# Four instead of two rounded weight buffers in a two-block transformer kernel, with a new order at its start

## The chip, the cores and the metric

The kernel runs on one core of one Trainium2 chip. Its time is the device time of one execution in microseconds. Before the change the median of three runs is 2723.0 us (2719.33 to 2724.44).

## The reference

Two transformer blocks are computed one after the other on one sequence of 256 tokens with a model width of 2048, all in float32. Each block has a modulation by a condition vector `c`, a mixer and a convolved feed-forward part of width 5632:

```python
mod = jax.nn.silu(c) @ w_ada[l] + b_ada[l]          # 2048 x 12288
shift_m, scale_m, gate_m, shift_f, scale_f, gate_f = jnp.split(mod[:, None, :], 6, axis=-1)
h = rms_norm(x, norm_mix_g[l]) * (1.0 + scale_m) + shift_m
proj = h @ w_in[l]
q, k, v, xs, z, bmat, cmat, dt_raw = jnp.split(proj, split_at, axis=-1)
...
mix = jnp.concatenate([attn, ssm], axis=-1) @ w_out[l]
x = x + gate_m * mix
h = rms_norm(x, norm_ffn_g[l]) * (1.0 + scale_f) + shift_f
x = x + gate_f * conv_ffn(h, w_up[l], conv_ffn_w[l], conv_ffn_b[l], w_down[l])
```

The first block's mixer has 8 attention heads with a relative bias and a state space part with 16 heads, whose time steps are `softplus(dt_raw + dt_bias)`. The second block's mixer has a recurrent part of 16 heads (8 pairs) with a state of 64 x 64 and a pooling part. A final norm ends each block.

## The kernel before, in words

**Weights.** All weights but the modulation's come as a stream of 376 units of 1 MB (128 partitions x 2048 values), numbered in the order of use. A unit goes through three steps. The SP queue loads it into `w_raw[:, u % 4]` (L362). ACT copies it, rounded, into `w_hi[:, u % 2]` (L1006 or L1011). DVE subtracts the copy and writes the rest into `w_lo[:, u % 4]`, which lies on the memory of `w_raw` (L1468 or L1472). The activations are split in the same way into `h_hi` and `h_lo`. PE then forms a product with three matmuls: high x high, high x low, low x high (L686 to L688), 48 for a unit. The counter `units_used` is u + 3 when unit u is done. The load of unit u waits for unit u - 4, and the rounded copy of unit u waits for unit u - 2, since there are two buffers.

**Modulation.** A row block of `w_ada` (1 MB) is multiplied by silu(c) and summed by one DVE instruction (L1484), which the text calls an `ada` sum; `ada_done` counts the sums. The first 32 sums, shift and scale of the first norm, come by the SP queue into the four slots of `first_raw` (L380), all later ones by the POOL queue into the two slots of `ada_raw` (L2012). The load of block q into `first_raw` waits for `ada_done >= q - 3`, that is until sum q - 4 is done; a load into `ada_raw` waits until the sum two before it is done. Each engine and each queue works in the order of its program, so whatever stands behind a waiting instruction waits too.

**Beginning.** The SP queue issues c, the parameters, two `ada` blocks, the constant `ones`, x, two `ada` blocks, units 0 and 1, the constants `ident` and `tri` and the bias table, and then for k = 2 to 15 the blocks 2k, 2k + 1 and unit k. ACT squares x, PE sums the squares (L683) once all three constants are there (`con_in >= 48`), and DVE and ACT make the norm's factor. Then a loop runs over k = 0 to 15, a turn for each tile of 128 channels. DVE's turn is:

```python
if k >= 2:
    first_ada(2 * k)
    first_ada(2 * k + 1)
...
# the channel's shift and gain, then tmp = x * gain * rstd
lo_unit(U_QK + k)
...
# h_lo[:, k] (L1597), once ACT has written h_hi[:, k]
```

ACT's turn is `h_hi[:, k]` and then `hi_unit(k + 1)`. PE multiplies unit k by tile k into all eight banks, which are q and k of the attention; ACT and DVE copy them to `qk` after unit 15.

**Input projection.** Eight chunks of four units follow (the first has one unit). In each, DVE writes the four `w_lo`, evacuates the chunk before (for chunks 1 to 3 with 12 convolution taps, L1616) and forms up to four `ada` sums, at places that the table `in1_ada` lists. After chunk 6's units it computes softplus by a series of 19 dependent instructions on 16 partitions (L1636 to L1648). State space part, attention and output projection follow. In attention, DVE forms four `ada` sums between the probabilities and the norm's variance (L1499).

**Second mixer.** `wkv_pe`, `wkv_act` and `wkv_dve` work on two head pairs at a time, i = 0 to 3. Five doubling steps (m, DVE L1386) invert a triangular matrix, a recurrence of four steps (q) carries the state, and the y phase normalizes the result. These steps are chains of small matmuls and DVE and ACT instructions, so PE has units of other projections between them (`pair(*units[n], ks=(a, b))` is the part a to b of unit n in eighths).

Of the kernel before, what the change touches and what calls it, by code (L numbers as in the profile page):

```python
# [20 lines left out]
P = 128  # L21
# [21 lines left out]
FFN_A, FFN_B = 12, 10  # L43
UNIT = 2048
# [122 lines left out]
def build_program(nc, a, out):  # L167
    with ExitStack() as ctx:
# [11 lines left out]
        w_hi = sb(ctx, "w_hi", [P, 2, UNIT], F32R)  # L180
# [8 lines left out]
        h_hi = sb(ctx, "h_hi", [P, KT, T], F32R)  # L189
        h_lo = sb(ctx, "h_lo", [P, KT, T], F32R)  # L190
# [9 lines left out]
        rstd = sb(ctx, "rstd", [P, 2, T])  # L200
        tmp = sb(ctx, "tmp", [P, 4, T])
# [5 lines left out]
        with ExitStack() as s:  # L207
            hid_hi = sb(s, "hid_hi", [P, 2 * FFN_A, T], F32R)
            hid_lo = sb(s, "hid_lo", [P, 2 * FFN_A, T], F32R)
            conv_y = sb(s, "conv_y", [P, 2, 4, T])  # L210
            silu_g = sb(s, "silu_g", [P, 2, T])
            prod = sb(s, "prod", [P, 2, T])
        with ExitStack() as s:
# [12 lines left out]
            with ExitStack() as t:  # L226
                bias = [sb(t, "bias", [P, 4, T]), bias_b]
                logit = [sb(t, "logit", [P, 4, 384]), logit_b]
                prob_t = [sb(t, "prob_t", [P, 4, 384]), prob_t_b]
# [3 lines left out]
            with ExitStack() as t:  # L233
# [4 lines left out]
                x_tok = sb(t, "x_tok", [P, 2, WIDTH])  # L238
                cb_t = sb(t, "cb_t", [P, 2, 384])
                lm = sb(t, "lm", [P, 4, 384])  # L240
        with ExitStack() as s:
# [15 lines left out]
            with ExitStack() as t:  # L257
# [9 lines left out]
                mv = [sb(t, f"mv{i}", [P, 2, 2, 64]) for i in range(2)]  # L267
# [3 lines left out]
        wtmp = [tmp, tmp_b]  # L271

# [84 lines left out]
        def _(sp):  # L357
# [150 lines left out]
        def wkv_pe(pe, mm, pair, i):  # L508
# [98 lines left out]
            for q in range(4):  # L607
# [15 lines left out]
                for s, g, b in both:  # L623
# [25 lines left out]
            if i != 2:  # L649
                pair(*units[5], ks=(0, 2))  # L650

# [3 lines left out]
            if i != 2:  # L655
                pair(*units[5], ks=(2, 4))
# [8 lines left out]
            if i != 2:  # L665
                pair(*units[5], ks=(4, 8))
# [5 lines left out]
        def _(pe):  # L672
# [17 lines left out]
            def chunk(u0, e0, n0, kind, n_all=UNITS, i0=0):  # L690
                def body(c, par_):
                    pe.wait_ge(act_evac, c + (e0 + 1))
                    pe.wait_ge(dve_evac, c + (e0 + 1))
                    for i in range(i0, 4):
                        pe.wait_ge(lo_ready, 4 * c + (u0 + i + 1))
                        pe.wait_ge(n_lo, min(n0 + (16 if kind == "tile" else 4 * i + 4), n_all))
                        w_h, w_l = w_hi[:, slot_of(i, u0) % 2], w_lo[:, slot_of(i, u0)]
# [24 lines left out]
            def down(u0, hc0, e_next, n):  # L722
# [4 lines left out]
                def body(b, first=False):  # L727
                    for i in range(4):
                        pe.wait_ge(hid_lo_s, 2 * b + (hc0 + i // 2 + 1))
                        pe.wait_ge(lo_ready, 4 * b + (u0 + i + 1))  # L730
                        w_h, w_l = w_hi[:, slot_of(i, u0) % 2], w_lo[:, slot_of(i, u0)]
# [17 lines left out]
            def pair(u, n, k0, first, n0=None, ks=(0, 8)):  # L749
# [4 lines left out]
                w_h, w_l = w_hi[:, u % 2], w_lo[:, u % 4]  # L754
# [10 lines left out]
            def lora_tile(i):  # L765
                u = U_LORA + i
                pe.wait_ge(lo_ready, u + 1)
                w_h, w_l = w_hi[:, u % 2], w_lo[:, u % 4]
# [8 lines left out]
            pe.wait_ge(con_in, 48)  # L777
            stat(0)
            for k in range(KT):
                pe.wait_ge(n_lo, N_H1 + k + 1)  # L780
                pe.wait_ge(lo_ready, U_QK + k + 1)
                w_h, w_l = w_hi[:, k % 2], w_lo[:, k % 4]
# [13 lines left out]
            pe.wait_ge(S("decays"), 1)  # L796
            for j in range(4):
# [108 lines left out]
        def wkv_act(act, A, hi_unit, evac, i):  # L906
# [42 lines left out]
            for m in range(5):  # L949
# [10 lines left out]
                if m == 2:  # L960
                    for s, g, b in both:
                        act.wait_ge(S("mv_mm"), g + 1)
                        nc.scalar.copy(mv[s][:].rearrange("p a b v -> p (a b v)"), ps[:, b, 0:T]).then_inc(S("mv"), 1)
# [32 lines left out]
        def _(act):  # L996
# [3 lines left out]
            def hi(c, i, u0):  # L1000
# [4 lines left out]
                act.wait_ge(units_used, 4 * c + (u0 + i + 1))  # L1005
                nc.scalar.copy(w_hi[:, slot % 2], w_raw[:, slot]).then_inc(hi_ready, 1)  # L1006
# [58 lines left out]
            stat(0, xs, 0)  # L1065
            hi_unit(U_QK)
            hi_unit(U_QK + 1)
            root(0)
# [388 lines left out]
        def _(dve):  # L1457
# [5 lines left out]
            def lo(c, i, u0):  # L1463
# [113 lines left out]
            for q in range(4):  # L1577
# [3 lines left out]
            for k in range(KT):  # L1581
                if k >= 2:
# [48 lines left out]
            def softplus():  # L1631
# [3 lines left out]
                dve.wait_ge(S("dt_exp"), 2)  # L1635
                steps.link(ts(SV, EV, 2.0, None, ALU.add))  # L1636
                steps.link(V.reciprocal(SV, SV))
                steps.link(tt(SV, SV, EV, ALU.mult))
                steps.link(tt(S2, SV, SV, ALU.mult))
                steps.link(ts(EV, S2, 1.0 / 19.0, None, ALU.mult))  # L1640
                for k in range(8, 0, -1):
                    steps.link(stt(out=EV, in0=EV, scalar=1.0 / (2 * k + 1), in1=S2, op0=ALU.add, op1=ALU.mult))
                steps.link(stt(out=EV, in0=EV, scalar=1.0, in1=SV, op0=ALU.add, op1=ALU.mult))
                steps.link(ts(XV, XV, 0.0, None, ALU.max))
                steps.link(stt(out=dtcs[:, 0], in0=EV, scalar=2.0, in1=XV, op0=ALU.mult, op1=ALU.add))
                steps.link(ts(SV, dtcs[:, 0], NA, -1.0, ALU.mult, ALU.mult))
                steps.link(V.memset(S2, 1.0))
                V.tensor_tensor_scan(dtcs[:, 1], S2, SV, 0.0, ALU.mult, ALU.add).then_inc(S("decays"), 1)  # L1648
# [9 lines left out]
            in1_ada = ((0, 0, 0, 1), (1, 1, 1, 1), (0, 1, 1, 1), (0, 1, 1, 1), (0, 1, 1, 1), (1, 1, 1, 1), (0, 1, 0, 1),  # L1658
                       (1, 1, 1, 1))
            for c in range(8):  # L1660
# [9 lines left out]
                if c == 6:  # L1670
                    softplus()
# [462 lines left out]
```

## Time and profile before

| | |
|---|---|
| median of 3 runs | 2723.0 us |
| runs | 2719.33, 2723.0, 2724.44 us |
| profiled execution | 2718.6 us |
| its span, first to last instruction | 2716.7 us |
| mean granted TensorE clock | 0.951 |

The profile is that of one execution, and its times count from the first instruction. PE is TensorE, DVE is VectorE, ACT is ScalarE, POOL is GpSimd; SPq is the queue in which SyncE issues transfers. A clock of 1.00 is 2.4 GHz and one of 0.50 is 1.2 GHz. A releaser, shown as `<-`, is what ended an engine's wait.

### The profile page before, as it was taken

How to read it: one execution, taken by the hardware profiler on the slowest of the kernel's cores; microseconds unless marked ns; L12 is line 12 of the kernel's file. 1: busy time of each engine (PE TensorE's matmuls, PEld its weight loads, DVE VectorE, ACT ScalarE, POOL GpSimd, SP SyncE). 2: the span in 40 equal slices, each digit the busy share in tenths (PEclk: the TensorE clock that was granted, in tenths of full speed). 3: DMA queues.
4: the chain of work that ended last, by engine and by line, in shares of the span. 5: the costliest groups of instructions: out<-in, count | busy, mean ns of one | idle time of the engine just before them, and what ended most of it. 6: DMA issues, size and time to landing. Idle time of an engine off the chain costs nothing.

```text
span 2716.7 us, 51420 instructions
## 1 busy us (share of the span) xinstructions
PE 2491.7 (92%) x21636; PEld 2411.4 (89%) x21636; DVE 1883.8 (69%) x2215; ACT 1114.1 (41%) x1179; POOL 87.8 (3%) x184
## 2 busy tenths in 40 slices
PE   4889885989999999999979999899899999999997
PEld 4888854989999999999969888789899999999997
DVE  5988768877777677776769766667777654555544
ACT  3234323345554334443343445333555433344433
POOL 0000000000000000000000000000000000000000
PEclk9999966999999999999989999899899999999999
DMA  7987723957776887777938422216576545455442
GB/s 318 392 337 278 283 115 134 367 219 278 278 287 242 332 287 275 277 278 282 329 138 325 159 85 85 99 64 235 213 270 243 184 171 185 170 186 178 177 171 108
DMA packets 87914, 613.56 MB, mean 226 GB/s; under 512 B 9576, under 2 KB 13168, under 8 KB 14320
## 3 DMA queue, kind: packets, MB, share of 16 engines
q1 hardware_dynamic: 64608, 442.95, 44.6%
q0 software_dynamic: 23184, 168.83, 16.1%
q8 instruction: 95, 1.56, 0.2%
q14 instruction: 27, 0.22, 0.0%
HBM read 607.54 MB, written 4.21 MB: 225 GB/s over the span
## 4 chain that ended last, share of the span: by engine, by line
PE 81%; DVE 12%; ACT 3%; issue 2%; DMA 1%; SPq 0%; DVEq 0%; ACTq 0%
PE ps L686 24%; PE ps L688 24%; PE ps L687 24%; DVE first_raw L1484 2%; PE ps L683 2%; DVE w_lo L1472 2%; ACT w_hi L1011 1%; DMA tri<-in_consts 1%; PE ps L573 1%; DVE w_lo L1468 1%; PE ps L818 1%; DVE rstd L1503 1%; PE ps L467 1%; DVE tmp L1511 1%; DVE xbc L1616 1%
## 5 line engine op out<-in xcount | busy, mean ns | idle before, releaser
L686 PE MATMUL ps<-h_hi,w_hi 128*128 128x256 f32 x4480 | 1288.3, 288 | 78.9 <-DVE h_lo L1597 28.3
L688 PE MATMUL ps<-h_hi,w_lo 128*128 128x256 f32 x4480 | 1278.6, 285 | 0.0
L687 PE MATMUL ps<-h_lo,w_hi 128*128 128x256 f32 x4480 | 1278.5, 285 | 0.0
L1468 DVE TENSOR_TENSOR w_lo<-w_raw,w_hi 128x2048 fp32r<-128x2048 f32 x307 | 703.7, 2292 | 534.8 <-ACT w_hi L1006 531.0
L1006 ACT CAST w_hi<-w_raw 128x2048 fp32r<-128x2048 f32 x306 | 583.5, 1907 | 1005.2 <-PE ps L688 972.2
L686 PEld LDWEIGHTS ps<-h_hi,w_hi 128*128 128x128 f32 x4480 | 871.2, 194 | 90.2 <-issue 33.6
L687 PEld LDWEIGHTS ps<-h_lo,w_hi 128*128 128x128 f32 x4480 | 871.6, 195 | 0.4
L688 PEld LDWEIGHTS ps<-h_hi,w_lo 128*128 128x128 f32 x4480 | 870.4, 194 | 0.0
L686 PE MATMUL ps<-hid_hi,w_hi 128*128 (+1 forms) x1408 | 397.3, 282 | 21.8 <-issue 21.8
L687 PE MATMUL ps<-hid_lo,w_hi 128*128 (+1 forms) x1408 | 396.6, 282 | 0.0
L688 PE MATMUL ps<-hid_hi,w_lo 128*128 (+1 forms) x1408 | 396.4, 282 | 0.0
L1484 DVE SCALAR_TENSOR_TENSOR ada_raw<-ada_raw,ada_c 128x2048 f32<-128x2048 f32 x160 | 365.3, 2285 | 9.1 <-DMA ada_raw<-in_ada_stream 9.1
L686 PEld LDWEIGHTS ps<-hid_hi,w_hi 128*128 128x128 f32 x1408 | 268.5, 191 | 22.5 <-issue 22.5
L687 PEld LDWEIGHTS ps<-hid_lo,w_hi 128*128 128x128 f32 x1408 | 268.5, 191 | 0.0
L688 PEld LDWEIGHTS ps<-hid_hi,w_lo 128*128 128x128 f32 x1408 | 268.3, 191 | 0.0
L1472 DVE TENSOR_TENSOR w_lo<-w_raw,w_hi 128x2048 fp32r<-128x2048 f32 x69 | 157.9, 2290 | 56.7 <-ACT w_hi L1011 56.2
L1011 ACT CAST w_hi<-w_raw 128x2048 fp32r<-128x2048 f32 x70 | 133.3, 1905 | 119.5 <-PE ps L688 114.8
L1784 DVE SCALAR_TENSOR_TENSOR conv_y<-ps,par,conv_y 128x254 f32<-128x254 f32 (+1 forms) x352 | 145.2, 475 | 18.8 <-ACT conv_y L1156 13.8
L2012 POOL DMA_DIRECT2D ada_raw<-in_ada_stream x160 | 84.6, 529 | 1940.0 <-DVE ada_raw L1484 1792.2
L683 PE MATMUL ps<-tmp,ones 128*128 128x256 f32 x224 | 65.9, 458 | 53.2 <-DMA tri<-in_consts 27.8
L683 PEld LDWEIGHTS ps<-tmp,ones 128*128 128x128 f32 x224 | 50.9, 233 | 64.6 <-DMA tri<-in_consts 27.8
L1156 ACT ACTIVATE conv_y<-ps,par 128x256 f32<-128x256 f32 x176 | 84.9, 563 | 15.2 <-PE ps L688 15.2
(331 smaller groups left out, 1531.8 us busy)
## 6 DMA issues: line engine op xcount, KB each, us to landing
w_raw<-in_w_stream SPq DMA_DIRECT2D x376, 1024.0 KB, 4.8
ada_raw<-in_ada_stream POOLq DMA_DIRECT2D x160, 1024.0 KB, 6.8
first_raw<-in_ada_stream SPq DMA_DIRECT2D x32, 1024.0 KB, 7.4
x<-in_x_t SPq DMA_DIRECT2D x1, 2048.0 KB, 13.8
x_kept<-x SPq DMA_DIRECT2D x1, 2048.0 KB, 7.3
out_t<-x SPq DMA_DIRECT2D x4, 512.0 KB, 2.7
ada_c<-in_c SPq DMA_DIRECT2D x1, 1024.0 KB, 4.4
ada_c<-in_c POOLq DMA_DIRECT2D x1, 1024.0 KB, 6.1
```

The source lines that it names most:

```text
L683: mm(bank(b), ones[:], tmp[:, q % 4], start=k == 0, stop=k == STATS[s] - 1).then_inc(sq_used, 1)
L686: mm(o, hi, r_hi, start=first, stop=False, **kw)
L687: mm(o, hi, r_lo, start=False, stop=False, **kw)
L688: return mm(o, lo, r_hi, start=False, stop=last, **kw)
L1006: nc.scalar.copy(w_hi[:, slot % 2], w_raw[:, slot]).then_inc(hi_ready, 1)
L1011: nc.scalar.copy(w_hi[:, u % 2], w_raw[:, u % 4]).then_inc(hi_ready, 1)
L1156: last = A(conv_y[:, par_, i], bank(4 * par_ + i), ACT.Identity, bias=pc(par_name, o + 3), scale=pc(par_name, o + 2))
L1468: tt(w_lo[:, slot], w_raw[:, slot], w_hi[:, slot % 2].bitcast(F32), ALU.subtract).then_inc(lo_ready, 1)
L1472: tt(w_lo[:, u % 4], w_raw[:, u % 4], w_hi[:, u % 2].bitcast(F32), ALU.subtract).then_inc(lo_ready, 1)
L1484: stt(out=rows, in0=rows, scalar=1.0, in1=ada_c[:], op0=ALU.mult, op1=ALU.mult, accum_out=col(mod, pair)).then_inc(ada_done, 1)
L1784: last = stt(out=conv_y[:, par_, i, d:T], in0=ps[:, 4 * par_ + i, 0:T - d], scalar=pc(par_name, o + 2 - d), in1=conv_y[:, par_, i, d:T], o ...
L2012: G.dma_start(ada_raw[:, slot], src).then_inc(ada_loaded[slot], 16)
```

## The change

`w_hi` gets four slots, so unit u has slot u % 4 in all three tiles, and a rounded copy waits for unit u - 4. For the memory, `prod` moves under `tmp`, `x_tok` and one `prob_t` under `h_lo`, and `mv` becomes a part of `wtmp`.

At the beginning the order of loads is new, PE's statistics wait for `ones` alone, DVE forms eight instead of four `ada` sums ahead of the loop and none in turns 0 to 3, and ACT takes the root ahead of the first two rounded copies. `first_raw` keeps its four slots and `load_first_ada` its wait.

Softplus is cut into three parts, put behind units (5, 3), (6, 0) and (6, 3). One `ada` sum leaves chunk 5, one moves within chunk 6, and attention gets a fifth. In the second mixer the sixth unit moves from the y phase into the four steps of the recurrence (for i = 0, 1 and 3).

```diff
-        w_hi = sb(ctx, "w_hi", [P, 2, UNIT], F32R)
+        w_hi = sb(ctx, "w_hi", [P, 4, UNIT], F32R)
...
+        with ExitStack() as under:
+            x_tok = sb(under, "x_tok", [P, 2, WIDTH])
+        with ExitStack() as under:
+            prob_t_a = sb(under, "prob_t", [P, 4, 384])
         h_lo = sb(ctx, "h_lo", [P, KT, T], F32R)
...
+        mv = [t[:, 1].rearrange("p (a b v) -> p a b v", a=2, b=2) for t in wtmp]
...
             sp.dma_start(ada_c[:], a["c"].partition_broadcast(P)).then_inc(c_in, 16)
-            sp.dma_start(par[:], a["params"]).then_inc(par_in, 16)
-            load_first_ada(0)
-            load_first_ada(1)
             sp.dma_start(ones[:], a["consts"][:, CCOL["ones"]:CCOL["ones"] + P]).then_inc(con_in, 16)
             sp.dma_start(x[:], a["x_t"]).then_inc(x_in, 16)
-            load_first_ada(2)
-            load_first_ada(3)
+            sp.dma_start(par[:], a["params"]).then_inc(par_in, 16)
+            for q in range(4):
+                load_first_ada(q)
             load_w(U_QK, 0, True)
-            load_w(U_QK + 1, 1, True)
+            for q in range(4, 2 * AHEAD):
+                load_first_ada(q)
+            for k in range(1, KT):
+                load_w(U_QK + k, k % 4, k < 4)
+                if k + AHEAD - 1 < KT:
+                    load_first_ada(2 * (k + AHEAD - 1))
+                    load_first_ada(2 * (k + AHEAD - 1) + 1)
             sp.dma_start(ident[:], a["consts"][:, CCOL["ident"]:CCOL["ident"] + P]).then_inc(con_in, 16)
             sp.dma_start(tri[:], a["consts"][:, CCOL["tri"]:CCOL["tri"] + T]).then_inc(con_in, 16)
             sp.dma_start(relb[:], a["rel_bias"]).then_inc(relb_in, 16)
-            for k in range(2, KT):
-                load_first_ada(2 * k)
-                load_first_ada(2 * k + 1)
-                load_w(U_QK + k, k % 4, k < 4)
...
+                if i != 2:
+                    pair(*units[5], ks=(2 * q, 2 * q + 2))
                 if q == 3:
                     break
...
-            if i != 2:
-                pair(*units[5], ks=(0, 2))
...
-            if i != 2:
-                pair(*units[5], ks=(2, 4))
...
-            if i != 2:
-                pair(*units[5], ks=(4, 8))
...
-            pe.wait_ge(con_in, 48)
+            pe.wait_ge(con_in, 16)
             stat(0)
...
             def hi_unit(u):
                 act.wait_ge(w_loaded[u % 4], 16 * (u // 4 + 1))
-                act.wait_ge(units_used, u + 1)
-                nc.scalar.copy(w_hi[:, u % 2], w_raw[:, u % 4]).then_inc(hi_ready, 1)
+                if u >= 4:
+                    act.wait_ge(units_used, u - 1)
+                nc.scalar.copy(w_hi[:, u % 4], w_raw[:, u % 4]).then_inc(hi_ready, 1)
...
             stat(0, xs, 0)
+            root(0)
             hi_unit(U_QK)
             hi_unit(U_QK + 1)
-            root(0)
...
-            for q in range(4):
+            for q in range(2 * AHEAD):
                 first_ada(q)
             var(0, D)
             inverse(0)
             for k in range(KT):
-                if k >= 2:
+                if k >= AHEAD:
                     first_ada(2 * k)
                     first_ada(2 * k + 1)
...
+            SOFTPLUS = {(5, 3): 0, (6, 0): 1, (6, 3): 2}
-            in1_ada = ((0, 0, 0, 1), (1, 1, 1, 1), (0, 1, 1, 1), (0, 1, 1, 1), (0, 1, 1, 1), (1, 1, 1, 1), (0, 1, 0, 1),
+            in1_ada = ((0, 0, 0, 1), (1, 1, 1, 1), (0, 1, 1, 1), (0, 1, 1, 1), (0, 1, 1, 1), (1, 1, 1, 0), (0, 1, 1, 0),
                        (1, 1, 1, 1))
...
-                if c == 6:
-                    softplus()
+                    if (c, i) in SOFTPLUS:
+                        softplus(SOFTPLUS[c, i])
...
-            next_ada(4)
+            next_ada(5)
```

`AHEAD` is 4. The same change of `hi_unit` is made in `hi`, and all readers of `w_hi` take slot u % 4.

## Rows read from the trace of the kernel before

**Rows 1.** Page, parts 1 and 2: span, and each engine's busy time (share) xinstructions.

```profile
span 2716.7 us, 51420 instructions
...
PE 2491.7 (92%) x21636; PEld 2411.4 (89%) x21636; DVE 1883.8 (69%) x2215; ACT 1114.1 (41%) x1179; POOL 87.8 (3%) x184
```

**Rows 2.** Waits of PE, whole span: engine line <- releaser: us in total, times, longest.

```profile
PE ps L686 <- DVE h_lo L1597: 28.3, 14, 9.3
PE ps L683 <- DMA tri<-in_consts: 27.8, 1, 27.8
...
PE ps L716 <- DVE w_lo L1468: 7.5, 1, 7.5
...
PE ps L686 <- DVE w_lo L1468: 6.6, 3, 2.2
```

**Rows 3.** Windows: width, busy us of PE, PEld, DVE, ACT, POOL, PEclk, DMA share, GB/s.

```profile
20.00:40.00 20.00, 10.22 (x32) 8.15 (x32) 4.77 (x5) 8.24 (x14) 2.49 (x19) 1.00 1.01 418
68.00:148.00 80.00, 65.88 (x494) 63.85 (x493) 79.31 (x91) 24.68 (x21) 0.00 (x0) 0.94 1.00 396
330.00:337.00 7.00, 6.77 (x21) 5.52 (x22) 7.00 (x5) 0.00 (x0) 0.53 (x1) 0.69 0.41 136
```

**Rows 4.** Timeline of DVE, one turn of the first loop: start, us, engine line op.

```profile
59.64 2.29 DVE L1484 SCALAR_TENSOR_TENSOR first_raw<-first_raw,ada_c 128x2048 f32<-128x2048 f32 x1
...
64.91 2.28 DVE L1472 TENSOR_TENSOR w_lo<-w_raw,w_hi 128x2048 fp32r<-128x2048 f32 x1
67.11 0.48 DVE L1597 SCALAR_TENSOR_TENSOR h_lo<-tmp,mod,h_hi 128x256 fp32r<-128x256 f32 x1
67.50 2.28 DVE L1484 SCALAR_TENSOR_TENSOR first_raw<-first_raw,ada_c 128x2048 f32<-128x2048 f32 x1
```

**Rows 5.** Timeline of the SP queue, first loop, turn k = 4's issues.

```profile
52.87 2.54 SPq L380 DMA_DIRECT2D first_raw<-in_ada_stream  x2
55.45 0.43 SPq L362 DMA_DIRECT2D w_raw<-in_w_stream  x1
```

**Rows 6.** Tile w_raw, 50 to 58 us: landing of the weight issued at 55.45.

```profile
DMA to landing us min/median/max: 8.7/8.7/8.7
```

**Rows 7.** DMA issues, first 1.3 us: KB each, us to landing.

```profile
ada_c<-in_c SPq DMA_DIRECT2D x1, 1024.0 KB, 4.4
```

**Rows 8.** Timeline of ACT: x has landed; third rounded copy; end of unit 15.

```profile
17.26 1.33 ACT L1024 ACTIVATE tmp<-x 128x256 f32<-128x256 f32 x4 [10.08 <-DMA x<-in_x_t]
...
55.10 1.90 ACT L1011 CAST w_hi<-w_raw 128x2048 fp32r<-128x2048 f32 x1 [6.52 <-PE ps L688]
...
168.08 1.93 ACT L1076 COPY qk<-ps 128x1024 f32<-128x1024 f32 x2 [5.91 <-PE ps L688]
```

**Rows 9.** Timeline of PE: start of unit 0.

```profile
47.36 0.58 PE L686 MATMUL ps<-h_hi,w_hi 128*128 128x256 f32 x1 [9.32 <-DVE h_lo L1597]
```

**Rows 10.** Timeline of DVE, chunk 2 of the input projection.

```profile
200.46 2.29 DVE L1468 TENSOR_TENSOR w_lo<-w_raw,w_hi 128x2048 fp32r<-128x2048 f32 x1 [3.45 <-ACT w_hi L1006]
202.67 5.02 DVE L1616 SCALAR_TENSOR_TENSOR xbc<-ps,par,xbc 128x255 f32<-128x255 f32 x12
```

**Rows 11.** Timeline of DVE, chunk 6: softplus, its longest step and the w_lo behind it.

```profile
318.60 1.74 DVE L1637 RECIPROCAL sp_w<-sp_w 16x256 f32<-16x256 f32 x1
...
327.72 2.25 DVE L1468 TENSOR_TENSOR w_lo<-w_raw,w_hi 128x2048 fp32r<-128x2048 f32 x1
```

**Rows 12.** Timeline of DVE, end of attention: last two sums, then variance.

```profile
454.68 2.29 DVE L1484 SCALAR_TENSOR_TENSOR ada_raw<-ada_raw,ada_c 128x2048 f32<-128x2048 f32 x1 [3.53 <-DMA ada_raw<-in_ada_stream]
...
457.67 2.29 DVE L1484 SCALAR_TENSOR_TENSOR ada_raw<-ada_raw,ada_c 128x2048 f32<-128x2048 f32 x1 [0.69 <-DMA ada_raw<-in_ada_stream]
...
460.68 0.42 DVE L1499 TENSOR_SCALAR rstd<-ps 128x256 f32<-128x256 f32 x1 [0.71 <-PE ps L683]
```

**Rows 13.** Timeline of DVE, fourth doubling step, i=1 and i=2.

```profile
1640.88 0.42 DVE L1386 TENSOR_TENSOR inv_t<-inv_t,ps 128x256 f32<-128x256 f32 x1 [1.39 <-PE ps L603]
...
1724.83 0.42 DVE L1386 TENSOR_TENSOR inv_t<-inv_t,ps 128x256 f32<-128x256 f32 x1 [3.94 <-PE ps L603]
```

More of the change, by code:

```diff
@@ L200, in build_program @@
         rstd = sb(ctx, "rstd", [P, 2, T])
+        with ExitStack() as under:
+            prod = sb(under, "prod", [P, 2, T])
         tmp = sb(ctx, "tmp", [P, 4, T])
@@ L228, in build_program @@
                 logit = [sb(t, "logit", [P, 4, 384]), logit_b]
-                prob_t = [sb(t, "prob_t", [P, 4, 384]), prob_t_b]
+                prob_t = [prob_t_a, prob_t_b]
                 att_m = [sb(t, f"att_m{b}", [P, 8]) for b in range(2)]
@@ L696, in body @@
                         pe.wait_ge(n_lo, min(n0 + (16 if kind == "tile" else 4 * i + 4), n_all))
-                        w_h, w_l = w_hi[:, slot_of(i, u0) % 2], w_lo[:, slot_of(i, u0)]
+                        w_h, w_l = w_hi[:, slot_of(i, u0)], w_lo[:, slot_of(i, u0)]
                         if kind == "tile":
@@ L730, in body @@
                         pe.wait_ge(lo_ready, 4 * b + (u0 + i + 1))
-                        w_h, w_l = w_hi[:, slot_of(i, u0) % 2], w_lo[:, slot_of(i, u0)]
+                        w_h, w_l = w_hi[:, slot_of(i, u0)], w_lo[:, slot_of(i, u0)]
                         for j in range(16):
@@ L753, in pair @@
                 pe.wait_ge(lo_ready, u + 1)
-                w_h, w_l = w_hi[:, u % 2], w_lo[:, u % 4]
+                w_h, w_l = w_hi[:, u % 4], w_lo[:, u % 4]
                 for k in range(*ks):
@@ L767, in lora_tile @@
                 pe.wait_ge(lo_ready, u + 1)
-                w_h, w_l = w_hi[:, u % 2], w_lo[:, u % 4]
+                w_h, w_l = w_hi[:, u % 4], w_lo[:, u % 4]
                 o = ps[:, (C_LORA + i // 2) % 2, (i % 2) * T:(i % 2) * T + T]
@@ L781, in _ @@
                 pe.wait_ge(lo_ready, U_QK + k + 1)
-                w_h, w_l = w_hi[:, k % 2], w_lo[:, k % 4]
+                w_h, w_l = w_hi[:, k % 4], w_lo[:, k % 4]
                 for j in range(16):
@@ L962, in wkv_act @@
                         act.wait_ge(S("mv_mm"), g + 1)
-                        nc.scalar.copy(mv[s][:].rearrange("p a b v -> p (a b v)"), ps[:, b, 0:T]).then_inc(S("mv"), 1)
+                        nc.scalar.copy(wtmp[s][:, 1], ps[:, b, 0:T]).then_inc(S("mv"), 1)
             for q in range(4):
@@ L1629, in in1_evac, with softplus @@
                     V.tensor_copy(v_tok[:, 1, o:o + 512], ps[:, 4 * par_ + 1, :]).then_inc(dve_evac, 1)
-            def softplus():
+            def softplus(part):
                 XV, EV, SV, S2 = (sp_w[:, i] for i in range(4))
                 NA = sp_w[:, 4, 0:1]
[L1635 to L1648, printed above, removed]
@@ new lines, in softplus @@
+                if part == 0:
+                    dve.wait_ge(S("dt_exp"), 2)
+                    steps.link(ts(SV, EV, 2.0, None, ALU.add))
+                    steps.link(V.reciprocal(SV, SV))
+                    steps.link(tt(SV, SV, EV, ALU.mult))
+                    steps.link(tt(S2, SV, SV, ALU.mult))
+                    steps.link(ts(EV, S2, 1.0 / 19.0, None, ALU.mult))
+                elif part == 1:
+                    for k in range(8, 0, -1):
+                        steps.link(stt(out=EV, in0=EV, scalar=1.0 / (2 * k + 1), in1=S2, op0=ALU.add, op1=ALU.mult))
+                else:
+                    steps.link(stt(out=EV, in0=EV, scalar=1.0, in1=SV, op0=ALU.add, op1=ALU.mult))
+                    steps.link(ts(XV, XV, 0.0, None, ALU.max))
+                    steps.link(stt(out=dtcs[:, 0], in0=EV, scalar=2.0, in1=XV, op0=ALU.mult, op1=ALU.add))
+                    steps.link(ts(SV, dtcs[:, 0], NA, -1.0, ALU.mult, ALU.mult))
+                    steps.link(V.memset(S2, 1.0))
+                    V.tensor_tensor_scan(dtcs[:, 1], S2, SV, 0.0, ALU.mult, ALU.add).then_inc(S("decays"), 1)
```

13 lines of the change are left out of this document (6 added, 7 removed).

## The prediction

> **What bounds the kernel now.** I read the page's busy shares first: PE works 92% of a span of 2716.7 us [rows 1]. So the change can save only where PE stands idle, and can lose wherever something else comes to set PE's pace. The list of PE's waits says where it stands idle. It names the constant `tri` (27.8 us in one piece, at the very start), `h_lo` of line 1597 (28.3 us over 14 waits, the first loop over `w_in`'s q and k columns), softplus in front of a `w_lo` (7.5 us) and three stalls of 2.2 us, 6.6 together, in the input projection [rows 2]. In the long streams of the feed-forward parts PE waits for no rounded weight at all. There a rounded copy that is ready earlier is worth nothing.
>
> The windows and timelines of the first 170 us then show what the new order acts on. From 68 to 148 us DVE is busy 79.31 of 80 us, while PE has 65.88 and the DMA engines are full [rows 3]. A turn of that loop takes 7.86 us (59.64 to 67.50). DVE forms two `ada` sums, then the small gain operations, starts `lo_unit` 5.27 us into the turn and `h_lo` 7.47 us into it [rows 4]. PE needs less per unit and waits.
>
> **The change, part by part.**
>
> *The start.* In the trace, `x` lands at 17.26 us behind 5780 KB (c, parameters, ones, two `ada` blocks and itself) [rows 8]. At the 418 GB/s of a full stretch [rows 3] these are 14.2 us, so 3.1 us lie around them. In the new order the eighth `ada` block is behind 12948 KB and lands at 31.7 + 3.1 = 34.8 us. DVE has summed it at 37.1, and statistics, root and reciprocal follow. Statistics no longer wait for `tri`, but the eighth sum comes later than they end, so only part of the 27.8 us comes back. `w3` is behind another 7168 KB and lands at 52.4. Its rounded copy (1.90 [rows 8]), `w_lo` (2.20, 64.91 to 67.11 [rows 4]) and `h_lo` (0.4) bring DVE to turn k = 4 at 56.9 us. Before it is 67.50 [rows 4]. Gain: 10.6 us. Four sums have moved out of the loop into time in which DVE waited, and turns 0 to 3 carry none.
>
> *The steady turns.* Here I expect the loss. The SP queue is in order, and I followed it against DVE's order. SP issues for k = 1, 2, ...: `load_w(k)`, then `ada` 2k+6 and 2k+7. But `first_raw` still has four slots, so `load_first_ada(q)` waits until sum q-4 is done. `ada` 2k+7 waits for sum 2k+3, which is the second sum of turn k+1. `load_w(k+1)` stands behind it in the queue. So from k = 4 on, `w_k` is issued only after both sums of turn k, and DVE's next large instruction in that same turn is `lo_unit(k)`, which needs `w_k` landed and rounded. In the kernel before, `w_k` stands behind `ada` 2k+1 instead, which waits for a sum of turn k-2, two turns of slack.
>
> The price of one such turn comes from a burst that the trace already has. At 52.87 and at about 55.1 us two `ada` blocks are issued into empty queues as sums finish, and the weight at 55.45, 2.58 us after the first [rows 5]. It lands 8.7 us after its issue, behind those two blocks [rows 6]. The first issue follows the first sum's start by 2.33 us (a sum is 2.29 [rows 4]). So in a new turn the weight is issued at 2.33 + 2.58 = 4.91 and lands at 13.6. The rounded copy adds 1.9 (15.5), `w_lo` 2.2 (17.7), `h_lo` 0.4 and two hand-overs make it 18.2 us against 7.86. This holds for k = 4 to 13, ten turns. After k = 12 no `ada` loads are left, so `w14` and `w15` are issued right behind `w13`, and turns 14 and 15 are of the old kind. Loss: 10 x (18.2 - 7.86) = 103.4 us. Nothing covers it: PE has each unit done within the turn, and four rounded buffers don't help, since no raw weight is there to be rounded.
>
> The bounds: if the two blocks ahead cost the weight nothing, it lands as the lone 1024 KB transfer of the start does, in 4.4 us [rows 7]. The turn is then 13.9 and the loss 60 us. From above, SP may issue or the blocks may land a little later: 1 us a turn more, 113 us. I take the burst, since it is the same sequence of three issues into idle queues.
>
> The Trainium skill (DMA: Bandwidth & Descriptors, Anatomy of one DMA) says that DMA engines don't wait on semaphores and that any wait is held on the issuing sequencer before dispatch, which is why a waiting `ada` load holds the weight behind it; it gives about 2.0 us fixed plus bytes at 436 GB/s. By that estimate three blocks from 2.33 us on would land at 2.33 + 2.0 + 7.2 = 11.5 us, a turn of 16.1 and a loss of 82 us. The row's 13.6 stands against it, and the sum goes by the row.
>
> *The last unit.* Unit 0 starts at 47.36 [rows 9] and is over when ACT is released at 55.10 [rows 8]: 7.7 us, from an idle PE. Unit 15 now takes 6.0 (`h_lo` of turn 15 starts at 67.50 + 11 x 7.86 + 7.47 = 161.4, PE 0.6 later, ACT is released at 168.08 [rows 8]). PE will idle some 10 us in every new turn, so I give the last unit 7.7: +1.7 us. The stage ends at 56.9 + 182 + 15.7 + 7.8 = 262.4 instead of 168.1. So +94.5 us in all, which is also -10.6 + 103.4 + 1.7.
>
> *Four rounded buffers in the input projection.* In a chunk with convolution DVE's `w_lo` at 200.46 waited 3.45 us for ACT's rounded copy, which waited for PE; then come 5.02 us of taps, and the `w_lo` behind them is late [rows 10]. With two more buffers that copy and its `w_lo` (1.9 + 2.2) are done before the chunk ends, so the taps start 2.2 us earlier (ACT's own part of the evacuation, 1.9, is then ahead of them). That removes 2.1 of each 2.2 us stall: -6.3.
>
> *Softplus in three parts.* Today it is a block on DVE, from before 318.60 to the next `w_lo` at 327.72 [rows 11], about 9.4 us, and PE waits 7.5 [rows 2]. Split over two chunks of some 22 us, in which DVE has 4 x 2.2 for weights and 2 or 3 sums, it fits: -7.5. The clock granted in 330 to 337 us is 0.69 [rows 3], behind that idle stretch; 0.31 / 0.5 x 7 = 4.3 us at 1.2 GHz cost 2.2 us, which come back: -2.2.
>
> *The fifth sum in attention.* The sums of `ada` there are paced by the POOL queue: the third starts at 454.68 after waiting 3.53 us for its block, the fourth at 457.67, and the variance follows at 460.68 [rows 12]. There are two slots, so a block is loaded only when the sum two before it is done. The second sum ended at 454.68 - 3.53 = 451.15 and the first 2.2 earlier, so these two blocks took 5.7 and 6.5 us. A fifth is issued at 454.68 + 2.3 = 457.0 and takes 6.2; its sum ends at 465.5. The variance sits behind it in DVE's order, and PE behind the norm: 465.5 - 460.7 = +4.8 us. The sum that was taken out of chunk 5 gives nothing, since DVE has slack there.
>
> *The sixth unit.* Its 48 matmuls move from the y phase into the four steps of the state recurrence, for i = 0, 1, 3. What such filler costs in a chain is shown by one doubling step: with 24 matmuls in it (i = 2) DVE waits 3.94 us, without (i = 1) 1.39 [rows 13]; so 24 cost 2.55 us, 48 about 5.1. What leaves the y phase is 5.8 us of PE time, of which its own waits hid some 2 to 3; a clock that stays up in the recurrence gives about 2 back. Net between -2 and +2 per i; I take +1 for all.
>
> *Memory and the rest.* `x_tok`, `prob_t` and `prod` lie on memory whose users have finished by the orders already there, and `mv` becomes a part of `wtmp`, dead at that step: 0. `ident`, `tri` and the bias table load after turn 15, some 90 us ahead of use: 0.
>
> **Sum.** +94.5 - 6.3 - 7.5 - 2.2 + 4.8 + 1 = +84.3 us. The profiled execution took 2718.6 us, of which 1.9 lie around the span; the median of the runs is 2723.0. The first gives 2803, the second 2807; I say 2805 us, +3.0%.
>
> **Rivals.** *A, faster: the order doesn't bind.* If `w_k` were issued in time (a sum of turn k did not stand ahead of it), the loop would keep 7.86 us per turn, and the rest would be -10.6 - 6.3 - 7.5 - 2.2 + 4.8 + 1 = -20.8: 2702 us. It decides when the weight is issued before about -1 us in its turn (4.4 + 1.9 before 5.27). For it speaks only that two loads of slack are there for k = 1 to 3; against it speaks the count of sums above. Chance 0.05. *B: the turn is short.* The weight lands in 4.4 us, the turn is 13.9, the loss 60 instead of 103: 2762 us. For it, the DMA queues are empty when the turn begins; against it, the 8.7 us of the burst [rows 6]. Values between come with it. Chance 0.14. *C: lost and won in balance.* Only a few turns wait, DVE catches up, and the time stays within 0.2%: it would take a stall of 2 us a turn where 10 are worked out. Chance 0.01. The forecast, 2785 to 2825 us, has 0.80.
>
> **The numbers.** The range of 8 in 10 takes the forecast and most of B: 2763 to 2825 us. The upper end has 1 us a turn more and half of the input projection's gains missing. Within 0.2%, about 5 us, is what measurement can't tell from no change. Faster 0.05, same 0.01, slower 0.94.
>
> **What would show it.** In the timeline of SP, ten weight issues 18 us apart, each right behind an `ada` issue. In DVE's idle time, about ten waits of 10 us for `w_hi`, and for `w_hi` a wait for the DMA of `w_raw`. The first copy of `qk` by ACT near 262 us, turn 4 near 57. No 2.2 us stalls and no 7.5 us stall behind it, and some 5 us more of idle PE ahead of the output projection. I am wrong if SP's weight issues come 8 us apart, or if the traffic lands much faster than the burst did.

## The result, and the profile after

The changed kernel takes 2783.55 us (median of 4 runs, 2780.39 to 2785.31), the kernel before 2721.16 us beside it: a ratio of 1.0227, with a 95% interval of 1.0209 to 1.0245. It is 62 us slower. The forecast was 2805 us, with a range of 2763 to 2825.

The page of the profiled execution (2780.39 us), which answers to [rows 1], with its chain that ended last:

```profile
span 2778.4 us, 51419 instructions
...
PE 2493.7 (90%) x21636; PEld 2415.7 (87%) x21636; DVE 1873.8 (67%) x2215; ACT 1112.0 (40%) x1179; POOL 99.2 (4%) x184
...
PE 78%; DVE 11%; DMA 5%; ACT 4%; issue 2%; SPq 0%; DVEq 0%; POOLq 0%; ACTq 0%
PE ps L686 23%; PE ps L687 23%; PE ps L688 23%; DMA w_raw<-in_w_stream 4%; DVE first_raw L1486 2%; PE ps L683 2%; ACT w_hi L1013 1%; DVE w_lo L1474 1%; DMA first_raw<-in_ada_stream 1%; PE ps L578 1%; PE ps L819 1%; PE ps L472 1%; DVE tmp L1513 1%; DVE xbc L1618 1%; PE ps L718 1%
```

The work is the same: no engine's busy time moved by more than 12 us, and the span grew by 61.7. So the loss is waiting. The chain says what for: the load of a weight, `w_raw`, is 4% of the span, and it isn't in this list of the kernel before. PE's waits, the answer to [rows 2]:

```profile
PE ps L686 <- DVE h_lo L1599: 111.6, 12, 21.9
...
PE ps L686 <- DVE w_lo L1470: 0.5, 1, 0.5
```

The wait for `tri`, the 7.5 us and the three of 2.2 us are gone. `h_lo` of the first loop has grown from 28.3 to 111.6 us. One of these waits, 21.9 us, is for the first tile, where PE waited for `tri` before; the others are those of the slow turns. The window over that loop's slow part, in the columns of [rows 3]:

```profile
57.00:230.00 173.00, 85.42 (x532) 83.39 (x530) 78.60 (x91) 24.74 (x21) 0.00 (x0) 0.72 0.50 194
```

DVE does in 173 us what it did in 80: the same 91 instructions, 78.60 us of work against 79.31 [rows 3]. The DMA engines work half of the time, and PE's clock is down to 0.72. Why no engine is busy is seen in one turn, followed over three timelines. First the SP queue, the answer to [rows 5]:

```profile
59.46 2.54 SPq L385 DMA_DIRECT2D first_raw<-in_ada_stream  x2
62.05 0.43 SPq L367 DMA_DIRECT2D w_raw<-in_w_stream  x1
...
112.42 2.54 SPq L385 DMA_DIRECT2D first_raw<-in_ada_stream  x2
115.01 0.43 SPq L367 DMA_DIRECT2D w_raw<-in_w_stream  x1
129.50 2.54 SPq L385 DMA_DIRECT2D first_raw<-in_ada_stream  x2
```

Then ACT (in its brackets: how long it sat idle, and what ended that), and DVE:

```profile
122.64 1.90 ACT L1013 CAST w_hi<-w_raw 128x2048 fp32r<-128x2048 f32 x1 [14.76 <-DMA w_raw<-in_w_stream]
```

```profile
110.10 2.28 DVE L1486 SCALAR_TENSOR_TENSOR first_raw<-first_raw,ada_c 128x2048 f32<-128x2048 f32 x1
...
124.57 2.29 DVE L1474 TENSOR_TENSOR w_lo<-w_raw,w_hi 128x2048 fp32r<-128x2048 f32 x1 [9.12 <-ACT w_hi L1013]
126.78 0.48 DVE L1599 SCALAR_TENSOR_TENSOR h_lo<-tmp,mod,h_hi 128x256 fp32r<-128x256 f32 x1
127.17 2.28 DVE L1486 SCALAR_TENSOR_TENSOR first_raw<-first_raw,ada_c 128x2048 f32<-128x2048 f32 x1
```

This is a closed ring. DVE begins its two sums at 110.10. Each sum frees a slot, SP issues the two `ada` blocks at 112.42 and 114.6, and only then the weight that stood behind them, at 115.01. It lands in 7.6 us. ACT rounds it at 122.64, DVE forms `w_lo` and `h_lo`, and at 127.17 the next two sums begin: a turn of 17.07 us. Each of the four (SP's order, the transfer, ACT, DVE) waits for the one before, and nothing of the next turn is under way.

DVE's waits from 57 to 230 us, the landing of the ten weights that stand behind two `ada` blocks (`w4` to `w13`), and the end of the stage, which was at 168.08 [rows 8]:

```profile
DVE w_lo L1474 <- ACT w_hi L1013: 93.7, 10, 10.6
```

```profile
DMA to landing us min/median/max: 7.0/7.8/9.1
```

```profile
252.35 1.93 ACT L1078 COPY qk<-ps 128x1024 f32<-128x1024 f32 x2 [6.42 <-PE ps L688]
```

DVE waits ten times, 93.7 us in all: this is the loss of the ten slow turns.

### The profile page after: what moved, and what is told of

Read it like the earlier page. It is cut to its first block, busy times and chain, and to the rows that moved or that the text cites. A ratio compares the mean times of both kernels' runs of the same rounds, so it can differ in the third digit from the quotient of the medians.

```text
span 2778.4 us, 51419 instructions
## 1 busy us (share of the span) xinstructions
PE 2493.7 (90%) x21636; PEld 2415.7 (87%) x21636; DVE 1873.8 (67%) x2215; ACT 1112.0 (40%) x1179; POOL 99.2 (4%) x184
## 4 chain that ended last, share of the span: by engine, by line
PE 78%; DVE 11%; DMA 5%; ACT 4%; issue 2%; SPq 0%; DVEq 0%; POOLq 0%; ACTq 0%
PE ps L686 23%; PE ps L687 23%; PE ps L688 23%; DMA w_raw<-in_w_stream 4%; DVE first_raw L1486 2%; PE ps L683 2%; ACT w_hi L1013 1%; DVE w_lo L1474 1%; DMA first_raw<-in_ada_stream 1%; PE ps L578 1%; PE ps L819 1%; PE ps L472 1%; DVE tmp L1513 1%; DVE xbc L1618 1%; PE ps L718 1%
## 5 line engine op out<-in xcount | busy, mean ns | idle before, releaser
L686 PE MATMUL ps<-h_hi,w_hi 128*128 128x256 f32 x4480 | 1298.2, 290 | 163.8 <-DVE h_lo L1599 111.6
```

The costliest lines, as they stand in the source:

```text
L686: mm(o, hi, r_hi, start=first, stop=False, **kw)
```

## The experiments

All times are compared with runs of the kernel before on the same chip, which gave medians of 2719.99 to 2720.75 us. "The changed kernel" is the one with the whole change.

**1. Where the loss sits: the two halves alone.** One kernel is the one before with only the new beginning (SP's order, four turns of sums ahead, `root(0)` first, `tri` later). One is the changed kernel with the beginning put back, to which this edit and SP's order belong:

```diff
-            for q in range(2 * AHEAD):
+            for q in range(4):
                 first_ada(q)
...
-                if k >= AHEAD:
+                if k >= 2:
```

A third has only four `w_hi` buffers and the memory moves that make room for them:

```diff
-        w_hi = sb(ctx, "w_hi", [P, 2, UNIT], F32R)
+        w_hi = sb(ctx, "w_hi", [P, 4, UNIT], F32R)
...
-                act.wait_ge(units_used, 4 * c + (u0 + i + 1))
-                nc.scalar.copy(w_hi[:, slot % 2], w_raw[:, slot]).then_inc(hi_ready, 1)
+                act.wait_ge(units_used, 4 * c + (u0 + i - 1))
+                nc.scalar.copy(w_hi[:, slot], w_raw[:, slot]).then_inc(hi_ready, 1)
```

New beginning alone:

> The kernel before (two rounded buffers, old softplus and sixth unit) with nothing but the new beginning. Theory S puts the whole loss there: the copy to qk starts near 252 us as in the changed kernel, +84 us, 2805 us. Rival N (the loss needs the four buffers, too): clearly less than that.

Measured: 2808.06 us, 1.0324 (1.0308 to 1.0340). Slower by 88 us, and the first copy of `qk` is at 259.7 us: the beginning is the whole loss.

Everything but the beginning:

> The new kernel with the whole old beginning (loads, eight sums, root, wait for the constants) and all other parts new. Theory S: the copy to qk starts near 168 us as in the kernel before, and the rest keeps its gain of 20 to 23 us: about 2700. Rival N (the four buffers themselves cost in the first loop, for instance by their memory or waits): the loop stays longer than 7.9 us a turn and the time is above 2723.

Measured: 2698.70 us, 0.9924 (0.9907 to 0.9941). The turns are of 7.87 us again, and the first copy of `qk` is at 167.15 us.

Four buffers alone:

> The kernel before with nothing but four rounded buffers and the memory moves. By the sum the three stalls of 2.2 us in the input projection go, -6.3, and some single waits with them: 2711 to 2715 us. Softplus' stall of 7.5 us stays. Rival: the buffers are worth nothing, since DVE sets the pace: 2721.

Measured: 2696.82 us, 0.9916 (0.9903 to 0.9930). That is a miss: 23 us gained where 6 to 10 were expected, and as much as everything but the beginning together. Where it comes from is read below.

**2. What in the beginning: the place of the weight in the queue.** Theory: each `w_k` is issued behind an `ada` block that waits for a sum of its own turn. Rivals: the burst of eight `ada` blocks at the start, or DMA bandwidth. Three orders of the same loads tell them apart. The first keeps the eight sums ahead of the loop, but loads `w1` to `w3` ahead of `ada` 8, and each later weight behind the two blocks of its own turn:

```diff
-            for k in range(1, KT):
-                load_w(U_QK + k, k % 4, k < 4)
-                if k + AHEAD - 1 < KT:
-                    load_first_ada(2 * (k + AHEAD - 1))
-                    load_first_ada(2 * (k + AHEAD - 1) + 1)
+            for k in range(1, 4):
+                load_w(U_QK + k, k, True)
+            for k in range(AHEAD, KT):
+                load_first_ada(2 * k)
+                load_first_ada(2 * k + 1)
+                load_w(U_QK + k, k % 4)
```

Here `w_k` stands behind `ada` 2k+1, which waits for a sum two turns back.

> Theory S (the SP order): w_k is late because it stands behind an ada block whose wait ends with a sum of the same turn. Here w1 to w3 are issued right after the eighth ada block and each later w_k behind ada 2k+1, so it has two turns of slack; nothing else of the new kernel changes. A turn of the first loop is 7.9 us again, the copy to qk starts near 154 us instead of 252.35, and the time falls from 2783.6 by about 99 to 2685 us, below the kernel before. Rival M (the transfers or the moved buffers are slower in the new kernel, whatever the order): turns stay above 12 us and the time above 2740.

Measured: 2686.16 us, 0.9872 (0.9856 to 0.9889). The first copy of `qk` is at 155.26 us.

The second has `w_k` behind `ada` 2k+3, with one turn of slack (the edit is against the first):

```diff
+            load_first_ada(8)
+            load_first_ada(9)
             for k in range(AHEAD, KT):
-                load_first_ada(2 * k)
-                load_first_ada(2 * k + 1)
+                if k + 1 < KT:
+                    load_first_ada(2 * (k + 1))
+                    load_first_ada(2 * (k + 1) + 1)
                 load_w(U_QK + k, k % 4)
```

> Theory S, as a dose: w_k stands behind ada 2k+3, so it is issued after the sums of turn k-1. It lands 4.9 + 8.0 = 12.9 us after that turn's start, is rounded at 14.8, and DVE wants it at 5.3 us into turn k. The turn then settles at 14.8 - 5.3 = 9.6 us (to 10.3 if it lands in 8.7), and the time is 17 to 24 us above that of the kernel with the weights first: 2702 to 2709. Rival M: no difference to the kernel with the weights first.

Measured: 2697.64 us, 0.9922 (0.9898 to 0.9946), 4 us under what was expected. The copy of `qk` is 14.6 us later than in the first.

The third puts `w_k` between the two `ada` blocks of the change, behind `ada` 2k+4 alone; `ada` 2k+5 follows it. Everything else is as in the changed kernel:

```diff
+            load_w(U_QK + 1, 1, True)
-            for k in range(1, KT):
-                load_w(U_QK + k, k % 4, k < 4)
-                if k + AHEAD - 1 < KT:
-                    load_first_ada(2 * (k + AHEAD - 1))
-                    load_first_ada(2 * (k + AHEAD - 1) + 1)
+            for k in range(2, KT):
+                if k + AHEAD - 2 < KT:
+                    load_first_ada(2 * (k + AHEAD - 2))
+                load_w(U_QK + k, k % 4, k < 4)
+                if k + AHEAD - 2 < KT:
+                    load_first_ada(2 * (k + AHEAD - 2) + 1)
```

> Theory S, the other dose: w_k changes places with the second ada block only, so it is issued after the first sum of its own turn (2.8 us into it) and lies behind one block, not two. It lands at about 9.8 us, the turn is 9.8 + 1.9 + 2.2 + 0.5 = 14.4 us against the 17.3 measured, over ten turns -29 us: about 2755. Rival M: the turn stays at 17.3, the time at 2784.

Measured: 2752.43 us, 1.0115 (1.0098 to 1.0132). The windows from 68 to 148 us, first with two turns of slack, then with one, then behind one block:

```profile
68.00:148.00 80.00, 69.60 (x541) 67.98 (x540) 78.50 (x91) 25.01 (x21) 7.34 (x11) 0.96 0.97 401
```

```profile
68.00:148.00 80.00, 63.29 (x447) 61.88 (x447) 67.44 (x75) 19.09 (x18) 0.00 (x0) 0.87 0.90 339
```

```profile
68.00:148.00 80.00, 45.74 (x294) 44.72 (x294) 45.34 (x54) 11.54 (x10) 0.00 (x0) 0.77 0.55 214
```

The same loads come at 401, 339 and 214 GB/s, so bandwidth isn't what limits the slow ones, and the burst at the start is in all three. What changes is how long SP holds the weight back. In the SP queue of the third kernel it is seen that the weight comes 0.4 us behind the first `ada` block and not behind the second, and that this turn is 14.1 us (86.19 to 100.28):

```profile
85.82 0.33 SPq L385 DMA_DIRECT2D first_raw<-in_ada_stream  x1
86.19 0.43 SPq L367 DMA_DIRECT2D w_raw<-in_w_stream  x1
88.03 12.21 SPq L385 DMA_DIRECT2D first_raw<-in_ada_stream  x2
100.28 0.43 SPq L367 DMA_DIRECT2D w_raw<-in_w_stream  x1
```

With one turn of slack DVE still waits 1.4 to 1.9 us in most turns, which are then 9.4 to 9.9 us:

```profile
87.38 2.29 DVE L1478 TENSOR_TENSOR w_lo<-w_raw,w_hi 128x2048 fp32r<-128x2048 f32 x1 [1.52 <-ACT w_hi L1017]
```

The median turn is 17.3, 14.2, 9.6 and 7.87 us for a weight that waits for the second sum of its own turn, for the first, for the turn before, and for two turns before. The theory holds at four points.

**3. Where four buffers gain.** The windows from 200 to 290 us, in the kernel before and in the one with four buffers alone:

```profile
200.00:290.00 90.00, 83.40 (x666) 82.79 (x666) 72.74 (x73) 39.65 (x36) 5.81 (x11) 0.96 0.77 288
```

```profile
200.00:290.00 90.00, 89.83 (x742) 89.18 (x742) 78.30 (x76) 41.27 (x34) 6.86 (x13) 1.00 0.88 328
```

Four buffers get 76 more matmuls into the same 90 us. At 90/742 = 0.121 us for each these are 9.2 us. The waits that went are 6.6 us [rows 2]. The rest is the clock, which is at 0.96 in the mean in the one window and at 1.00 in the other: it fell behind two of the three stalls. The kernel before, over one stall and what follows it:

```profile
262.00:264.00 2.00, 0.42 (x4) 0.22 (x2) 2.00 (x3) 1.49 (x1) 0.53 (x1) 1.00 0.31 41
264.00:266.00 2.00, 1.38 (x11) 1.39 (x12) 2.00 (x2) 0.41 (x1) 0.00 (x0) 1.00 0.79 332
266.00:268.00 2.00, 2.00 (x12) 2.00 (x11) 2.00 (x3) 0.00 (x0) 0.53 (x1) 0.53 1.00 401
268.00:270.00 2.00, 2.00 (x13) 2.00 (x12) 0.97 (x1) 0.00 (x0) 0.00 (x0) 0.62 0.99 385
270.00:272.00 2.00, 2.00 (x19) 2.00 (x18) 1.86 (x1) 0.00 (x0) 0.00 (x0) 1.00 0.96 369
```

Some 3 us at 1.2 GHz follow 2.2 us of rest, and 12 and 13 matmuls are done in 2 us instead of 19. By the granted clock that is 0.47 x 2 + 0.38 x 2 = 1.7 us for this stall. Another stall, up to 237.64 us, cost the same (0.70, 0.50 and 0.94 in the three windows from 238 us on). The third, up to 212.15 us, cost nothing (1.00 in each 2 us behind it). So the three are worth 6.6 us of waits and, by the two readings, 2.6 to 3.4 us of slow clock: 9 to 10 us.

Softplus gives a second part. In the kernel with four buffers alone it is one block as before, but PE waits 3.3 us at it instead of 7.5 [rows 2], which fits PE having more weights ready to work on:

```profile
PE ps L721 <- DVE w_lo L1475: 3.3, 1, 3.3
```

What the split is then still worth was measured with the weights first and four sums in attention, softplus as one block and then in three parts, on one chip (the edit that puts the block back; one sum of chunk 6 moves with it):

```diff
-                    if (c, i) in SOFTPLUS:
-                        softplus(SOFTPLUS[c, i])
+                if c == 6:
+                    softplus()
```

> The kernel with the weights loaded first and four sums in the attention's turn, but softplus as one block on DVE again (the sum in the sixth chunk's last but one place goes back with it); the sixth unit stays where the change put it. Open is what the split of softplus was worth. Theory 1, my forecast's: it takes away the whole wait of 7.5 us and 2.2 us of slow clock behind it, so putting the block back costs 9.7 us: 2689. Theory 2, after the run with four buffers alone, where PE's wait at softplus had shrunk to 3.3 us: rounded weights further ahead already cover half of the block, and only 3.3 us are left to the split: 2683. Theory 3: weights that come earlier cover all of it: 2680, no difference to the split kernel.

> The kernel with the weights loaded first and four sums in the attention's turn once more, as the partner of the one with softplus in one block, on the same chip. Expected is its former time, 2680 us and 0.986 of the kernel before, by all theories; the difference of the two is read.

Measured: 2682.87 us (0.9869, 0.9852 to 0.9886) in one block, 2681.50 us (0.9862, 0.9845 to 0.9878) in three. PE's wait ahead of the output projection's first `w_lo`, one block and three parts:

```profile
PE ps L717 <- DVE w_lo L1471: 3.9, 1, 3.9
```

```profile
PE ps L717 <- DVE w_lo L1471: 0.2, 1, 0.2
```

The wait of 3.7 us is taken away, about as the second theory said. From the first copy of `qk` to the variance behind attention the two traces take 275.8 and 272.1 us, 3.7 apart as well. Behind that the order is the other way round by 1.8 us, less than what one kernel scatters there (see below). In the time the split shows as 1.4 us, which the intervals don't tell from nothing. The first theory (9.7 us) is wrong.

**4. The fifth sum, and the sixth unit.** With the weights first, the fourth sum goes back to chunk 5:

```diff
-(1, 1, 1, 0), (0, 1, 1, 0),
+(1, 1, 1, 1), (0, 1, 1, 0),
...
-            next_ada(5)
+            next_ada(4)
```

> The kernel with the weights first and, in addition, the fourth sum back in chunk 5 beside softplus' first part, so that attention has four sums again. By the sum the fifth cost 4.8 us (the variance came 4.1 us later in the changed kernel's trace); chunk 5 has the room. 2682 us. Rival: the sum in chunk 5 makes DVE late for its weights and gives the 4 us back: 2686.

Measured: 2679.82 us, 0.9857 (0.9842 to 0.9872). Then the sixth unit goes back to the y phase as well:

```diff
-                if i != 2:
-                    pair(*units[5], ks=(2 * q, 2 * q + 2))
...
+            if i != 2:
+                pair(*units[5], ks=(0, 2))
```

> The kernel of the run before this one with the sixth unit back in the y phase. My sum gave the new place +1 us in all; the changed kernel's trace has the head pairs' stages 2 to 4 us shorter than before, of which the buffers may hold a part. If the sixth unit's place did it, this is 2 to 4 us slower, 2684 to 2686; if the sum was right, the same as or 1 us below the run before.

Measured: 2679.57 us, 0.9852 (0.9837 to 0.9868). The place of the sixth unit is worth nothing that these runs can tell.

On the fifth sum: the kernel with four sums stands at 0.9857 and, in its second run (experiment 3), at 0.9862, the one with five at 0.9872; the intervals overlap, so the time alone doesn't carry it. The trace does. The last sums of attention in the changed kernel, the answer to [rows 12]:

```profile
522.87 2.29 DVE L1486 SCALAR_TENSOR_TENSOR ada_raw<-ada_raw,ada_c 128x2048 f32<-128x2048 f32 x1 [0.42 <-DMA ada_raw<-in_ada_stream]
...
528.23 2.29 DVE L1486 SCALAR_TENSOR_TENSOR ada_raw<-ada_raw,ada_c 128x2048 f32<-128x2048 f32 x1 [3.06 <-DMA ada_raw<-in_ada_stream]
...
530.45 0.42 DVE L1501 TENSOR_SCALAR rstd<-ps 128x256 f32<-128x256 f32 x1
```

The fifth sum waits 3.06 us for its block and the variance starts in the moment in which it ends. From the last evacuation of the input projection (`v_tok`) to this variance the kernel before takes 106.45 us (354.23 to 460.68 [rows 12]), the changed one 110.68 (419.77 to 530.45). In the five kernels with five sums it is 110.0 to 111.6 us, in the seven with four 103.0 to 107.3. PE shows it, too: its wait for the first `h_lo` behind this norm is 10.4 to 11.5 us with five sums and 6.1 to 6.8 with four. So the fifth sum is real: 4.2 us against the kernel before, 5 us between the means of the two groups. Kernel before and changed kernel:

```profile
PE ps L686 <- DVE h_lo L1515: 6.1, 1, 6.1
```

```profile
PE ps L686 <- DVE h_lo L1517: 10.4, 1, 10.4
```

**5. The beginning needs the four buffers.** In the kernel with the new beginning alone, turn k = 4 begins at 61.76 us and not at 57.14. ACT's rounded copy for it waits there for PE, since there are only two buffers:

```profile
57.22 1.91 ACT L1013 CAST w_hi<-w_raw 128x2048 fp32r<-128x2048 f32 x1 [3.44 <-PE ps L689]
```

```profile
61.76 2.28 DVE L1486 SCALAR_TENSOR_TENSOR first_raw<-first_raw,ada_c 128x2048 f32<-128x2048 f32 x1
```

The first copy of `qk` is at 259.7 us there and at 252.35 in the changed kernel: 4.6 of these 7.3 us are the later start, the rest turns of 17.6 instead of 17.3 us. With the old beginning the new parts gain only 0.9 us in this stage. So in the profiled spans the halves don't add up: the new beginning alone is +91.5 us, everything else alone -20.3, and together they are +61.7, not +71.2; some 6 us of the gap lie in this stage. In the medians the gap is smaller, +88 and -22 against +62, since the profiled execution of the changed kernel is the fastest of its runs and that of the new beginning alone the slowest.

## Why the prediction came out as it did

The direction and the mechanism were right, and the time lay in the range, 21 us below the figure. It lay 1.5 us below the likeliest case's own 2785 to 2825, in the part of the range that was there for rival B, whose short landing didn't happen. So that the range held is in part luck: the loss was forecast too large and the gains too small, and all the larger misses point the same way. The terms, measured along the path (one milestone in both traces for each; the fourth row is the sum of the three above it):

| term | forecast | measured |
|---|---|---|
| start, turn k = 4 | -10.6 | -10.4 (67.50 and 57.14) |
| ten slow turns | +103.4 | +94.7 (17.3 each) |
| last unit | +1.7 | 0 |
| end of the QK stage | +94.5 | +84.3 (168.08 and 252.35) |
| input projection with softplus | -16.0 | -18.7 (354.23 and 419.77) |
| fifth sum | +4.8 | +4.2 (460.68 and 530.45) |
| all that follows | +1 | -8.0 (2704.49 and 2766.22) |
| sum | +84.3 | +61.7 |

A pair of times is where the row's part ends before and after: the start of turn 4, the first copy of `qk`, the last `v_tok`, the variance behind attention, and the last variance. The last row but one rests on the last variance of the kernel, first before and then after:

```profile
2704.49 0.42 DVE L1499 TENSOR_SCALAR rstd<-ps 128x256 f32<-128x256 f32 x1 [4.88 <-PE ps L683]
```

```profile
2766.22 0.42 DVE L1501 TENSOR_SCALAR rstd<-ps 128x256 f32<-128x256 f32 x1 [4.89 <-PE ps L683]
```

*The start* was right within 0.2 us (turn 4 at 57.14, forecast 56.9), and *the queue* to the tenth: the first weight, at 62.05, is issued 4.91 us into its turn, as forecast. Three orders of the same loads confirm the mechanism, and the kernel with two turns of slack has the old turn, 7.87 us.

*The ten turns* are the term that was mis-sized. The forecast took the landing of one burst, 8.7 us [rows 6], for every turn. The ten landings are 7.0 to 9.1 us, median 7.8, and a turn takes 17.3 us and not 18.2; ten of them are worth 8.7 us. The burst's 8.7 lies within this spread: one reading stood for all ten. The estimate from the Trainium skill (DMA: Bandwidth & Descriptors, Anatomy of one DMA), a turn of 16.1 us, erred by 1.2 us on the other side; the page gives its figures for transfers issued by GpSimd, and these are issued by SyncE. Rival B, a landing of 4.4 us as of a lone block, is wrong: behind one block (experiment 2) the median is 7.0 us, behind two 7.8.

*The last unit* costs nothing: from the end of DVE's part to ACT's release it takes 6.1 us in both kernels. The forecast gave it the time of a unit behind an idle PE, but turns 14 and 15 are of the old kind, and the granted clock is 1.00 again from 236 us on (0.51 from 230 to 236).

*Four buffers* were undersized, and this is a step of the reasoning that failed. "That removes 2.1 of each 2.2 us stall: -6.3" counted the waits and not the slow clock behind them, 2.6 to 3.4 us more. They also take 4.2 of softplus' 7.5 us, which the forecast gave to the split. Alone, four buffers give 23 us in the medians and 18.7 in the spans, and not 6.3. Along the path of that trace it is 1.8 up to the first copy of `qk`, 13.9 in the input projection (9 to 10 and 4.2 of it are explained above), -0.9 in attention and 3.8 behind it.

*Softplus in three parts*: the wait of 7.5 us went, but half of it by the buffers. The split alone removes a wait of 3.7 us and moves the time by 1.4, within what the runs scatter.

*The sixth unit*: 0.3 us between the medians, where +1 was forecast; no row priced the 2 to 3 us of hidden waits and the 2 us of clock in that sum. PE's waits do shift with it: with the unit in its new place it waits 5.0 us instead of 2.1 for `x` in the second output projection, and the total is the same.

*The rest of the kernel*: "There a rounded copy that is ready earlier is worth nothing" holds in the feed-forward streams, which take 793.5 to 796 us each, with two buffers or four. It doesn't hold in what lies between them. From attention's variance to the last variance the two kernels with two buffers take 2243.8 and 2243.7 us; the ten traces of kernels with four have 2235.8 to 2242.3, 2239.2 in the mean: 4.6 us less. One wait behind it is seen, in the second output projection. Both kernels with two buffers have it, and none of the ten traces with four. In the kernel before it reads:

```profile
PE ps L683 <- ACT tmp L1273: 3.9, 1, 3.9
```

PE waits there for ACT's squares of the last two tiles of `x`, and these come at the end of a chain:

```profile
1903.33 1.90 ACT L1011 CAST w_hi<-w_raw 128x2048 fp32r<-128x2048 f32 x1 [0.83 <-PE ps L688]
1908.37 0.72 ACT L1273 ACTIVATE tmp<-x 128x256 f32<-128x256 f32 x2 [3.15 <-DVE x L1919]
```

```profile
1905.26 2.29 DVE L1472 TENSOR_TENSOR w_lo<-w_raw,w_hi 128x2048 fp32r<-128x2048 f32 x1 [3.52 <-ACT w_hi L1011]
1907.46 0.87 DVE L1919 SCALAR_TENSOR_TENSOR x<-ps,mod,x 128x256 f32<-128x256 f32 x2
```

With two buffers the rounded copy waits for PE, DVE's `w_lo` waits for the copy, and DVE's last sums into `x` stand behind `w_lo`. With four buffers the copy doesn't wait for PE, and those sums wait for PE alone (0.85 us in the kernel with four buffers alone). That the wait went is read from the traces; that it is the whole 4.6 us is not shown. Open is the rest of the -8.0: the changed kernel is the lowest of the ten, and one kernel profiled twice gives 2236.6 and 2240.1, so 3.5 us are scatter.

The kernel that follows from this, the change with the weights first and four sums in attention, takes 2680 to 2682 us, 1.4% less than the kernel before and 3.7% less than the changed one.

## What to carry to other kernels

In an in-order load queue a load that waits for a free slot holds everything behind it, so count the slack of each load from the waits of the loads ahead of it: here the order of the same loads alone decided between 2.3% slower and 1.3% faster. A short stall of the bounding engine costs more than its length where the clock falls behind it. One landing read from a trace is one of a spread (here 7.0 to 9.1 us), so a price that is multiplied by ten wants several. Edits that relieve the same stall don't add up, so each is measured alone and with the others.

## What the hardware showed that was not expected

- PE's clock fell to 1.2 GHz (granted 0.53 and 0.62 in two windows of 2 us) behind a rest of only 2.2 us in two of three places, and not in the third.
- The weight behind two 1024 KB blocks landed in 7.0 to 9.1 us (median 7.8) in the changed kernel, in 9.9 to 13.2 us (median 11.6, `w6` to `w15`) in the faster kernel with two turns of slack. There the DMA engines are at 0.97 of their time, and the longer landing costs nothing, because the load is issued earlier.
- A 1024 KB load takes 7.0 us (median) behind one block and 7.8 behind two, so the second block ahead seems to cost only 0.8 us, where 1024 KB need 2.5 us at the 418 GB/s of [rows 3]. Most of that is the head start: by the SP rows the first block is issued 0.4 us ahead of the weight in the one case (where a second block follows 1.8 us behind it) and 2.6 us in the other. Counted from the first block's issue the weight lands after 7.4 and 10.4 us, 3.0 apart. `w4` in the kernel with two turns of slack, which has no block right ahead of it, landed in 4.8 us.
